# TensorE's expert loop written out for all pairs, and a pooled branch computed features-first, in a one-core encoder

## What is computed

```
h = rmsnorm(x);  u, q, k, v, o, gates = h @ W_in
y_pool  = concat_g( (window_mean_g(u_g) - u_g) @ pool_w[g] ) * pool_scale     # 256 features, 4 windows
y_mlstm = gated, normed bidirectional mLSTM(q, k, v, gates)                   # 768 features, 4 heads
x = x + concat(y_pool, y_mlstm) @ W_out
x = x + expert_choice_SwiGLU(rmsnorm(x))    # 16 experts, each takes its 34 + 130 best tokens
y = rmsnorm(x)
```

## Time and profile before

| | us |
|---|---|
| median of 3 runs | 1764.13 (1763.55 to 1764.77) |
| the profiled execution | 1767.92 |
| its span, first to last instruction | 1766.1 |
| PE busy | 1735.0 |
| VectorE, ScalarE, GpSimd busy | 420.5, 383.8, 298.4 |

### The profile page before, as it was taken

How to read it: one execution, slowest core, us unless ns; L and a number is a source line. 1 busy time by engine, 2 the same in 40 slices (tenths; PEclk the granted TensorE clock), 3 DMA queues, 4 the chain that set the end, 5 groups by cost and what they waited for, 6 DMA issues and landing times.

```text
span 1766.1 us, 25121 instructions
## 1 busy us (share of the span) xinstructions
PE 1735.0 (98%) x10359; PEld 1403.2 (79%) x10359; DVE 420.5 (24%) x987; ACT 383.8 (22%) x890; POOL 298.4 (17%) x330
## 2 busy tenths in 40 slices
PE   9999999999999999999999999999999999999996
PEld 5556556855555774555899999999999999999996
DVE  4562113621020560069201101011010110101105
ACT  3335224332131533455000000000000000000005
POOL 0080022520101253443000010100101001010010
PEclk9999999999999999999999999999999999999998
DMA  9211012321110535534577676876859758587585
GB/s 297 78 51 52 20 36 76 90 89 36 36 39 18 163 101 182 177 99 154 197 251 278 214 250 232 294 250 211 279 205 310 261 187 283 212 307 255 181 278 227
DMA packets 178721, 307.28 MB, mean 174 GB/s; under 512 B 11068, under 2 KB 63468, under 8 KB 178528
## 3 DMA queue, kind: packets, MB, share of 16 engines
q1 hardware_dynamic: 171408, 283.30, 46.5%
q0 software_dynamic: 7248, 23.09, 5.2%
HBM read 275.02 MB, written 31.35 MB: 173 GB/s over the span
## 4 chain that ended last, share of the span: by engine, by line
PE 95%; ACT 1%; DVE 1%; DMA 1%; issue 1%; SPq 0%; POOL 0%; DVEq 0%; ACTq 0%; POOLq 0%
PE bank L2118 32%; PE bank L2138 16%; PE bank L1890 12%; PE bank L1867 9%; PE bank L2019 8%; PE bank L1801 3%; PE bank L1837 2%; PE bank L1953 2%; PE bank L1934 1%; PE bank L1849 1%; PE bank L1846 1%; PE bank L1845 1%; PE bank L2162 1%; PE bank L2093 1%; PE bank L1972 1%; PE bank L1943 1%
## 5 line engine op out<-in xcount | busy, mean ns | idle before, releaser
L2118 PE MATMUL bank<-arena 128*128 128x164 f32 x4096 | 579.7, 303 | 0.3 <-DVE arena L1658 0.3
L2118 PEld LDWEIGHTS bank<-arena 128*128 128x128 f32 x4096 | 571.8, 190 | 0.5 <-DVE arena L1658 0.5
L2138 PE MATMUL bank<-arena 128*128 128x164 f32 x2048 | 296.4, 303 | 0.4 <-DVE arena L1669 0.4
L2138 PEld LDWEIGHTS bank<-arena 128*128 128x128 f32 x2048 | 286.7, 190 | 0.6 <-DVE arena L1669 0.6
L1890 PE MATMUL bank<-arena 128*128 128x512 f32 (+1 forms) x576 | 214.0, 534 | 0.0
L1890 PEld LDWEIGHTS bank<-arena 128*128 128x128 f32 x576 | 110.0, 191 | 102.5 <-issue 92.7
L1669 DVE TENSOR_TENSOR arena<-bank,arena 128x328 f32<-128x328 f32 x64 | 32.0, 500 | 655.8 <-ACT arena L1241 655.8
L821 POOL DMA_INDIRECT residual<-arena,cur_scatter x30 | 44.9, 1497 | 691.3 <-DVE arena L1678 633.8
L1867 PE MATMUL bank<-arena 128*128 128x384 f32 x480 | 155.7, 485 | 0.0
L1241 ACT ACTIVATE arena<-bank 128x328 f32<-128x328 f32 x64 | 28.4, 443 | 558.5 <-PE bank L2118 558.5
L2019 PE MATMUL bank<-arena 128*128 128x512 f32 x320 | 146.0, 599 | 0.8 <-issue 0.8
(11 more groups left out here) (273 smaller groups left out, 1504.2 us busy)
## 6 DMA issues: line engine op xcount, KB each, us to landing
arena<-in_w_up SPq DMA_DIRECT2D x32, 2048.0 KB, 14.7
arena<-in_w_down SPq DMA_DIRECT2D x32, 2048.0 KB, 10.3
arena<-in_w_gate SPq DMA_DIRECT2D x32, 2048.0 KB, 8.3
arena<-in_w_in SPq DMA_DIRECT2D x7, 1536.0 KB, 6.5
arena<-in_x_sample SPq DMA_DIRECT2D x14, 512.0 KB, 5.9
arena<-x_features_first SPq DMA_DIRECT2D x11, 512.0 KB, 7.8
arena<-decay_rows SPq DMA_DIRECT2D x22, 256.0 KB, 4.6
arena<-state_rows SPq DMA_DIRECT2D x44, 128.0 KB, 4.0
```

Source lines behind the costliest of these rows:

```text
L2118: last = pe.matmul(ps[2 * w + fp % 2][:, a * SLOTS:(a + 1) * SLOTS], ring[2 * (fp // 2) + w][:, k, f * P:(f + 1) * P], xeT[:, k, SIDE[side ...
L2138: last = pe.matmul(to, ring[4 + dp // 2][:, k, dt * P:(dt + 1) * P], hidT[:, k, :], start=k == 0, stop=k == KT - 1)
```

## The change

1. PE's loop over the seven passes becomes a Python loop that writes the passes out one after the other, with waits on constants. The loops of the other engines stay.
2. The pooled product has its operands exchanged: the pool weights are stationary and up to 512 tokens of `mixed[j]` are moving. The result is features-first; it is stored as `pool_features` (256 x T) in HBM. `mixer_out` keeps only the 384 columns of the first pair of heads.
3. In the projection the pooled half of a tile is loaded by a DMA of its own, `load_pool`, into the first 256 columns of `y_t`, features-first, and is used there as the stationary operand of k = 0, 1. Only six blocks of y are turned, and ScalarE copies 256 columns less. `transpose_y` waits for both loads (32 in place of 16). `load_pool(n + 2)` waits until the second projection of step n is done, and stands behind `load_x3(n + 2)` in SP's program.

```diff
@@ encoder_program
-    y_d = nc.dram_tensor("mixer_out", (T, Y_W), F32, kind="Internal").ap()
+    y_d = nc.dram_tensor("mixer_out", (T, PAIR), F32, kind="Internal").ap()
+    pool_d = nc.dram_tensor("pool_features", (2 * P, T), F32, kind="Internal").ap()
...
-            sp.dma_start(y_t[n % 2], y_d[i * P:(i + 1) * P, :]).then_inc(y_in[n % 2], 16)
+            sp.dma_start(y_t[n % 2][:, D_POOL:Y_W], y_d[i * P:(i + 1) * P, :]).then_inc(y_in[n % 2], 16)
+
+        def load_pool(sp, n):
+
+            if n >= 2:
+                multiplied(sp, ("wo", n - 2, 1))
+            pooled = y_t[n % 2][:, 0:D_POOL].rearrange("p (j t) -> p j t", j=2)
+            sp.dma_start(pooled, pool_d.rearrange("(j p) t -> p j t", p=P)[:, :, tile_cols(ORDER_B[n])]).then_inc(y_in[n % 2], 16)
...
-                            sp.dma_start(y_d[:, j * P:(j + 1) * P].rearrange("(i p) n -> p i n", p=P),
-                                         ypool[j].rearrange("p (i n) -> p i n", n=P)).then_inc(ypool_out, 16)
+                            sp.dma_start(pool_d[j * P:(j + 1) * P, :], ypool[j]).then_inc(ypool_out, 16)
...
-                        sp.dma_start(y_d[:, D_POOL:D_POOL + PAIR].rearrange("(i p) n -> p i n", p=P),
+                        sp.dma_start(y_d.rearrange("(i p) n -> p i n", p=P),
...
                 for n in range(2):
                     load_y(sp, n)
+                    load_pool(sp, n)
                     load_x3(sp, n)
...
                     if n + 2 < NT:
                         load_y(sp, n + 2)
                         load_x3(sp, n + 2)
+                        load_pool(sp, n + 2)
...
-                def move(key, out, parts=P, w=512):
+                def move(key, out, parts=P, w=512, at=0):
                     multiplied(act, key)
-                    act.activation(out, ps[plan[key][0]][0:parts, 0:w], ACT.Copy).then_inc(free[plan[key][0]], 1)
+                    act.activation(out, ps[plan[key][0]][0:parts, at:w], ACT.Copy).then_inc(free[plan[key][0]], 1)
 
                 def halves(name, n, slots):
                     for h in range(2):
-                        move((name, n, h), slots[n % 2][:, 512 * h:512 * h + 512])
+                        lo = D_POOL if name == "yT" and h == 0 else 512 * h
+                        move((name, n, h), slots[n % 2][:, lo:512 * h + 512], at=lo - 512 * h)
...
                                 for g in range(3):
                                     b = bank(("po", j, g))
-                                    for a in range(4 * g, min(4 * g + 4, NT)):
-                                        c = (a - 4 * g) * P
-                                        last = pe.matmul(ps[b][:, c:c + P], src[:, tile_cols(a)], pw[:, j, :], start=True, stop=True)
-                                    last.then_inc(full[b], 1)
+                                    lo, hi = 512 * g, min(512 * g + 512, T)
+                                    pe.matmul(ps[b][:, 0:hi - lo], pw[:, j, :], src[:, lo:hi], start=True, stop=True).then_inc(full[b], 1)
...
-                        for k in range(4):
+                        for k in range(D_POOL // P if name == "yT" and h == 0 else 0, 4):
                             last = pe.transpose(ps[b][:, k * P:(k + 1) * P], source(4 * h + k), ident[:, :])
...
-                    pe.wait_ge(y_in[n % 2], 16 * (n // 2 + 1))
+                    pe.wait_ge(y_in[n % 2], 32 * (n // 2 + 1))
...
+                def mixer(n, k):
+
+                    return (y_t if k * P < D_POOL else yT_t)[n % 2][:, k * P:(k + 1) * P]
+
...
-                        last = pe.matmul(ps[b][:, :], yT_t[n % 2][:, k * P:(k + 1) * P], wout[:, k, 512 * h:512 * h + 512],
+                        last = pe.matmul(ps[b][:, :], mixer(n, k), wout[:, k, 512 * h:512 * h + 512],
...
-                with pe.Fori(0, PAIRS - 1) as i:
+                for i in range(PAIRS - 1):
```

More of the change, by code:

```diff
@@ L2013, in project @@
                             for g in range(QUARTERS):
-                                last = pe.matmul(ps[b][g * TAIL:(g + 1) * TAIL, 0:w], yT_t[n % 2][:, k * P:k * P + TAIL],
+                                last = pe.matmul(ps[b][g * TAIL:(g + 1) * TAIL, 0:w], mixer(n, k)[:, 0:TAIL],
                                                  wout[:, k, 512 * h + g * w:512 * h + (g + 1) * w], start=k == 0, stop=k == KT - 1)
```

## The result

The changed kernel took 1771.03 us (median of 8 runs, 1769.21 to 1774.27) against 1765.11 us before (8 runs, 1763.55 to 1767.82): ratio 1.003, 95% interval 1.002 to 1.004, slower by 5.9 us. The forecast was 4.8 us slower, 1768.9 us, range 1764.5 to 1771.8. It was added to 1764.13 us, the median of three runs of the kernel before; eight runs give 1765.11, so 1.0 of the 2.1 us by which 1771.03 lies above 1768.9 comes from there.

A forecast was written before the change was run, and what follows sets the result against it. TensorE (PE), busy 1735.0 of 1766.1 us, was taken as the bound. The terms 0 - 0.2 - 2.4 + 5.6 + 1.0 + 0.8 = +4.8 us gave 1768.9 us, range 1764.5 to 1771.8.

The forecast's parts named there:

- Part 1: PE's expert loop written out: jumps back cost nothing and fetches of new instructions stay hidden, 0 us.
- Rival C: Expert loop: each of six jumps back costs a fetch hidden in PE's busy time; 13 us gain, chance 0.04.
- Part 2: Pooled product on PE: 12 instructions in place of 44 stream the same columns, 0.2 us saved.
- Part 3: Output projection: six blocks of y transposed per tile instead of eight, 22 fewer transposes, 2.4 us saved.
- Part 4: Pooled load in the projection: PE waits 5.6 us at the short tile, 1.0 us one tile on; others hidden.
- The clock: PE idle before the transposes of y(9) lowers its granted clock: 0.8 us lost, bounds 0 and 1.8.
- Rival B: Late-issued pooled load lands fast, clock stays up: not slower, +0.6 us, up to +3.4; chance 0.28.
- Rival D: Expert passes 2 to 7: instruction fetches come late behind expert weights, adding 6 us, 1775; chance 0.03.

The follow-up runs named there:

- e5: Changed kernel with the pooled load ahead of the x load and on its own semaphore, waited for before the projection reading it: 1763.29 us, ratio 0.9988 to before.
- e3: Changed kernel with the pooled load put ahead of the x load in SP's loop: 1764.63 us, ratio 0.9993 to the kernel before.
- e7: Changed kernel with the pooled load one place further back, behind the store of the sum: 1806.18 us, ratio 1.0227 to the kernel before.

## Why the prediction was right, and where it was not

**Part 1, the loop: 0 us.** Right for the kernel before (ratio 1.0003), and the passes and the q8 count (82; I said near 83) came as written. But it was priced against the kernel before alone. Beside the pooled branch, which shifts the loop, writing it out is worth some 12 us (1782.80 against 1771.03). I read that pass 2 fetched nothing and took that for a property of the loop; it is one of the loop at its place. The sum holds because both parts were in it: neither kernel compared has the refetch. Rival C, which I gave 0.04, named a fetch at each jump back for a program that was not on either side; its 13 us came close, but from a load's 2.2 us and with the fetch hidden inside PE's busy time, where it shows as idle time and on q8. That the forecast's 0 held for the pair is partly luck: with the loop kept, the pooled branch would have cost 17 us, and nothing in the prediction would have said so.

**Part 2, the pooled product: 0.2 us.** Right: 4.91 us became 4.73 us.

**Part 3, the transposes: 2.4 us.** Right: 0.66 us for six against 0.87 for eight; a gap of 0.21 in each of 11 tiles, and ordinary tiles are 16.26 us apart (691.90 to 708.16), where I had said 16.25. It is worth that much while TensorE ends the stage last, as here; e5 shows less.

**Part 4, the new load.** Right in place and order. The wait at the short tile is 5.71 us, for which I had 5.6; the second 0.85 us, for which I had 1.0. The load was issued 0.9 us after PE could have used it, and landed 4.8 us after its issue (4.2 to 4.4 in the other profiles of this order), behind the x loads; e3 and e7 show, by moving it, that what stands in front sets the landing. One term that I put at nothing was not: the 0.41 us for which PE waited on ScalarE at 794.22 are gone in the changed kernel, whose transposes at 794.66 follow without a wait, 0.4 us in its favour. That ordinary tiles hide it is right: there are two waits, not eleven.

**The clock.** Right in kind, undersized: 1.7 us measured in one execution, inside the bounds of 0 and 1.8, and 2.4 in another, outside them; I took 0.8. I had reckoned that part of the slow stretch would fall on work that it does not slow; in fact all 14 transposes lay in it, and in the second execution most of the short projection behind them.

**Sum.** 5.7 + 0.9 + 1.7 - 2.4 - 0.4 = 5.5 us for the stage by the terms measured, against 5.65 between the two traces; the pooled product takes 0.2 off. The medians say 5.9, with an interval of some 3.5 to 7. The 1.1 us between forecast and median lie within that; of the terms, the clock is the one that was most off, by 0.9 us or more. Rival B fell: the landing came 4.8 us after issue and not 2.2, the clock did not stay up. Rival D did not occur: the fetches of the passes written out cost nothing.

## What to carry to other kernels

When a transfer is added, find the waits ahead of it in its queue, not only its own, and compare its issue time with the time at which the consumer arrives at the shortest step of the loop; give it its own semaphore, and wait where the data is read. Count what an edit does to the length of the program ahead of a long loop: a loop on the engine that is kept in one position can be fetched anew in every pass in another, and a look at the instruction queue's traffic in pass 2 shows which it is. A part that is worth nothing against the kernel before can still be worth 12 us beside the other parts.

## What was not expected of the hardware

A loop of PE of about 1700 instructions ran its second pass without any fetch or with nine blocks of 16 KB by nothing but its position; the second case costs 1.0 to 1.7 us in pass 1 and 2.0 to 2.5 us in each pass after it, at the jump back and just behind it. Waits that were long satisfied were not free: 74 instructions of two waits each left PE idle for 5.8 to 5.9 us, some 80 ns an instruction by an estimate from these numbers, and the granted clock behind them was 0.69 and 0.50. The 148 of them made the stage 11.5 us longer.
